# One number of the placement table: where VectorE normalises the second row block's differential heads

## The reference

```python
h = _rmsnorm(x, pre_norm_g[i])
z = h @ w_in[i]
qa, ka, va, qi, ki, wi, ga, qb, kb, vb, gb = _split_in(z)
qa = _partial_rope(...); ka = _partial_rope(...)      # 8 heads of 64, 16 columns rotated
oa = _dsa_attention(qa, ka, va, qi, ki, wi, top_k)    # top 64 keys of each query
qb = _partial_rope(...); kb = _partial_rope(...)
# (softmax(Q1 K1) - lam * softmax(Q2 K2)) V, then an RMS norm over each head's 128 columns
ob = _rmsnorm(_diff_out, subln_g[i]) * (1.0 - lam_init)
y = concatenate([oa * silu(ga), ob * silu(gb)]) @ w_out[i]
x = x + _rmsnorm(y, post_norm_g[i])
e = (p[i] @ w_ple_proj[i]) * sigmoid(x @ w_ple_gate[i])
x = x + _rmsnorm(e, ple_norm_g[i])
```

## Time and profile before

| | us |
|---|---|
| median of 3 runs (367.97 to 368.6) | 368.36 |
| the profiled execution's own time | 368.36 |
| its span | 366.6 |
| PE busy | 354.2 (97%) |
| DVE busy | 265.0 (72%) |
| ACT busy | 227.5 (62%) |
| POOL busy | 69.0 (19%) |

### The profile page before, as it was taken

One profiled execution on the slowest core, in us unless ns is written; L12 is line 12 of the kernel. 1 busy time (PEld: TensorE's weight loads), 2 busy tenths in 40 slices (PEclk: granted clock), 3 DMA queues, 4 the chain that ended last, 5 costly groups with the idle time before them and its releaser, 6 DMA issues.

```text
span 366.6 us, 5649 instructions
## 1 busy us (share of the span) xinstructions
PE 354.2 (97%) x1908; PEld 291.9 (80%) x1908; DVE 265.0 (72%) x554; ACT 227.5 (62%) x455; POOL 69.0 (19%) x121
## 2 busy tenths in 40 slices
PE   7799999999999999999999999999999999999992
PEld 6597788788887878888888877878888788888881
DVE  2666798879975586687697478878997658668543
ACT  4667565875867953664584547588586795366221
POOL 1514522023600000004005612203360000000000
PEclk9899999999999999999999999999999999999998
DMA  7999836354585364467754845646457436540011
GB/s 255 319 217 322 308 116 183 116 160 130 166 239 169 116 194 163 154 214 138 213 168 139 279 121 167 172 117 176 121 168 244 154 115 219 165 161 32 0 53 63
DMA packets 32076, 61.65 MB, mean 168 GB/s; under 512 B 2384, under 2 KB 4688, under 8 KB 32048
## 3 DMA queue, kind: packets, MB, share of 16 engines
q1 hardware_dynamic: 30928, 58.01, 50.3%
q0 software_dynamic: 1120, 3.28, 4.4%
HBM read 60.23 MB, written 1.05 MB: 167 GB/s over the span
## 4 chain that ended last, share of the span: by engine, by line
PE 90%; issue 2%; DMA 2%; POOL 2%; DVE 1%; ACT 1%; SPq 0%; DVEq 0%; POOLq 0%
PE proj L983 26%; PE proj L985 25%; PE proj L984 25%; PE sc L1087 3%; PE sc L1028 3%; PE tr L1100 2%; DMA g_norm<-in_pre_norm_g_dram 2%; PE tr L1044 2%; PE pv L1121 2%; PE pv L1116 1%; PE sc L1058 1%; POOL v_all L470 1%; DVE work L755 0%; DVE w_lo L716 0%; PE tr L1035 0%
## 5 line engine op out<-in xcount | busy, mean ns | idle before, releaser
L983 PE MATMUL proj<-w_hi,act_hi 128*128 128x512 f32 (+1 forms) x416 | 166.2, 400 | 0.2 <-DVE act_lo L768 0.2
L985 PE MATMUL proj<-w_hi,act_lo 128*128 128x512 f32 (+1 forms) x416 | 160.3, 385 | 0.0
L984 PE MATMUL proj<-w_lo,act_hi 128*128 128x512 f32 (+1 forms) x416 | 159.8, 384 | 0.0
L716 DVE TENSOR_TENSOR w_lo<-raw,w_hi 128x1024 fp32r<-128x1024 f32 (+1 forms) x108 | 129.4, 1213 | 21.3 <-ACT w_hi L529 20.4
L529 ACT ACTIVATE w_hi<-raw 128x1024 fp32r<-128x1024 f32 (+1 forms) x108 | 109.4, 1032 | 5.8 <-DMA raw<-in_w_in_dram 4.0
L983 PEld LDWEIGHTS proj<-w_hi,act_hi 128*128 128x128 f32 x416 | 78.2, 188 | 16.2 <-issue 1.1
L985 PEld LDWEIGHTS proj<-w_hi,act_lo 128*128 128x128 f32 x416 | 78.1, 188 | 15.9
L984 PEld LDWEIGHTS proj<-w_lo,act_hi 128*128 128x128 f32 x416 | 78.3, 188 | 12.9
L477 POOL TENSOR_TENSOR rstd<-var,minus_half 128x1 f32<-128x1 f32 x12 | 6.7, 554 | 183.8 <-DVE var L706 168.6
L630 ACT ACTIVATE probs<-probs,neg_max 128x128 f32<-128x128 f32 (+1 forms) x64 | 28.2, 446 | 3.3 <-DVE neg_max L839 3.2
L529 ACT ACTIVATE pT<-tr 128x512 f32<-128x512 f32 (+1 forms) x22 | 12.7, 575 | 17.4 <-PE tr L1100 15.5
(11 more groups left out here) (126 smaller groups left out, 390.9 us busy)
## 6 DMA issues: line engine op xcount, KB each, us to landing
raw<-in_w_in_dram SPq DMA_DIRECT2D x64, 512.0 KB, 3.9
raw<-in_w_out_dram SPq DMA_DIRECT2D x16, 512.0 KB, 3.3
raw<-in_w_ple_gate_dram SPq DMA_DIRECT2D x16, 512.0 KB, 3.6
raw<-in_w_in_dram SPq DMA_DIRECT2D x8, 324.0 KB, 6.8
raw<-in_w_ple_proj_dram SPq DMA_DIRECT2D x4, 512.0 KB, 3.5
resid<-in_x_dram SPq DMA_DIRECT2D x2, 512.0 KB, 7.3
g_norm<-in_post_norm_g_dram POOLq DMA_DIRECT2D x2, 512.0 KB, 6.0
g_ple<-in_ple_norm_g_dram POOLq DMA_DIRECT2D x2, 512.0 KB, 7.1
```

The lines of the kernel that those rows point to most:

```text
L716: nc.vector.tensor_tensor(w_lo[:, g % SLOTS, 0:nk * cols], raw[:, g % RAW_SLOTS, 0:nk * cols], w_hi[:, g % SLOTS, 0:nk * cols].bitcast(fp3 ...
L983: nc.tensor.matmul(ps, src_hi[:, b, k0 + k, :], hi, start=(first_u and k == 0), stop=False)
L984: nc.tensor.matmul(ps, src_hi[:, b, k0 + k, :], lo, start=False, stop=False)
L985: last = nc.tensor.matmul(ps, src_lo[:, b, k0 + k, :], hi, start=False, stop=last_k)
```

## The change

One number. The step `hn` of row block 1 moves from behind piece 29 to behind piece 31, in both layers.

```diff
     hv=[21, 27],
-    hn=[23, 29],
+    hn=[23, 31],
     topk=[[0, 0, 2, 6, 6, 7, 10, 11], [12, 24, 24, 25, 26, 26, 27, 31]],
```

## The result

| | before | after |
|---|---|---|
| median of 6 runs each, on one chip, us | 368.48 | 370.94 |
| lowest to highest | 367.77 to 369.20 | 370.09 to 371.37 |
| ratio, 95% interval | | 1.0065 [1.0049, 1.0083] |
| the profiled execution, us (span) | 368.36 (366.6) | 371.55 (369.8) |

The changed kernel is slower by 2.46 us. The forecast was 370.5, in a range of 369.7 to 371.3.

The account below looks back on a forecast made before the run. PE was taken to bound the kernel from 30 us on. Moved normalisation 0, earlier subtractions 0, a PE stop of 1.09 us in each of two layers: 368.36 + 2.2 = 370.5 us, range 369.7 to 371.3.

Parts of the forecast that it names:

- What bounds: From 30 us to the last matmul PE sets the time, and any stop of PE is kept to the end.
- The moved normalisation: On DVE, five operations of 1.23 us end some 2.5 us later; PE needs them twelve pieces later; cost 0.
- The subtractions earlier: On DVE, two subtractions start 1.23 us earlier; the transfers and matmuls they release have nobody waiting; gain 0.
- The rotation's delay: On POOL, two subtractions meet the rotation of KA's block 0 and add 2.06 us to it.
- The stop: PE's transposes of KA's block 0 start at 99.11 instead of 98.02: 1.09 us lost in each layer.
- The first start: DVE starts at 95.31, POOL at 95.36; if POOL is first, the stop differs by a tenth.
- the pair of subtractions of the earlier trace: Two DVE subtractions taking 2.54 us, set against 2.85 beside POOL's second rotation to show that they stretched.
- The upper bound: Longest holds on POOL's rotation, its third operation held too: 2.31 us delay, 1.34 stop, 2.7 for both layers, 371.0.
- the longer wait: A held POOL operation goes on only about 115 ns behind DVE's end; 1.2 us more for both layers, 371.7; not adopted.
- keep its turn: Rival: only the rotation's first operation is held, about 1.0 us, PE late by a few hundredths, 368.4; chance 0.09.
- The second rotation: POOL's rotation of KA's block 1 loses its 1.79 us of delay; rival faster by 0 to a few tenths, chance 0.02.
- The clock: Rival: PE's granted clock falls behind the stop, about 1.7 us more lost a layer, about 374; chance 0.04.

Follow-up runs that it names:

- Experiment 4: The kernel before with the normalisation moved to 31 in layer 0 alone, layer 1 left at 29: 369.98 us, ratio 1.0037.
- experiment 3: The changed kernel with PE's transposes of KA's block 0 one piece later (KA=[34, 37]): 369.05 us, ratio 1.0004.
- experiment 2: The kernel before with the normalisation moved to 33, three more DVE steps later than in the changed kernel: 371.23 us, ratio 1.0074.

## Why the prediction was right

**What bounds.** PE, once the start is over, and it keeps every stop. Experiment 4 shows the adding, and experiment 3 that nothing but PE's stops counts. "From 30 us on" was read off one trace: in six of the ten PE waits for a `w_lo` between 31 and 34 us, so the start reaches a little further.

**The moved normalisation, cost 0.** Right: experiment 2 moves it further at no price.

**The subtractions earlier, gain 0.** Right as far as it shows: experiment 3 has them as early as the changed kernel, without the stops, and stands at 1.0004.

**The rotation's delay.** Forecast 2.06 us, read off another pair in the trace; measured 3.56 - 1.54 = 2.02. **The stop:** forecast 1.09 in each layer, measured 1.05 and 1.04, the 0.15 from POOL to PE included. The first start, with DVE ahead by 0.03 to 0.05, went to DVE in every trace that has the new order; POOL first was not met. One comparison of the prediction has a wrong base: the pair of subtractions of the earlier trace rows runs beside a rotation too. Where POOL does nothing, in the kernel before, a pair takes 2.35:

```profile
129.84 2.35 DVE L716 TENSOR_TENSOR w_lo<-raw,w_hi 128x1024 fp32r<-128x1024 f32 x2
```

Beside a rotation pairs take 2.54, 2.62 and 2.85, so POOL lengthens a pair by 0.2 to 0.5; the exclusion goes both ways, as the prediction says, and its sum doesn't use this number. The upper bound let `scale_h` hold the rotation's third operation; that one was plain (0.31), and `scale_h` was the one that took longer.

On when the held operation goes on, the rows speak against the longer wait. The first subtraction alone has this row in the changed kernel:

```profile
96.31 1.21 DVE L716 TENSOR_TENSOR w_lo<-raw,w_hi 128x1024 fp32r<-128x1024 f32 x1
```

It ends at 97.52. The operation of POOL that it holds ends at 97.85, so its own 0.46, if that is its plain time once it goes on, began at 97.39, or 0.13 ahead of the reported end. The Trainium skill (SBUF — State Buffer, "A bandwidth-pool intuition that's wrong (but worth ruling out)") gives about 115 ns behind the end, a figure measured on a DMA's descriptor generation. For these two compute engines the trace doesn't agree: by it each of two holds would be 0.25 longer and the rotation's delay about 2.5, where 2.02 was measured. The prediction took 199.86 for the end of the subtraction in the earlier trace rows, as half of a pair whose second half is the longer; the difference is a few hundredths and changes nothing in this.

**The total.** 2.18 forecast, 2.46 measured, with an interval of 1.8 to 3.1. The 0.3 between them has no place in the traces, where the two landmarks of the table lie 2.22 further apart, and it is within the noise: against the two larger sets of the kernel before, 369.00 and 368.42, the 31 runs on record of the changed kernel, median 370.81, are slower by 1.8 and 2.4. That the forecast is right to a few tenths is therefore worth less than that each of its terms was found.

**The rivals.** The rotation doesn't keep its turn: two operations in a row are held. The second rotation was freed, as expected, and nobody waits for it. The clock did not fall in the stop, in which PE, long busy before, paused for about 1 us; here is the stretch of the earlier trace rows in the changed kernel, where PE lost 0.90 of busy time and the granted clock stayed at 1.00:

```profile
95.00:110.00 15.00, 14.10 (x77) 11.22 (x76) 13.78 (x35) 8.78 (x18) 4.97 (x8) 1.00 0.70 204
```

## What to carry to other kernels

Before moving work on VectorE, put GpSimd's timeline beside it. Here a 128x1024 subtraction with two SBUF inputs and an operation of GpSimd took turns (each operation held by a whole subtraction lasted 0.8 to 1.1 us longer), while a normalisation that reads PSUM and a multiplication that writes its sum left GpSimd at its plain times. So a move that leaves both queues' work unchanged can still lengthen a chain on the other engine. Look for who waits soonest behind what is newly hit, and compare the slack there with the delay; here 1.1 us of slack stood against 2.0 of delay, and with one instruction less in the way 0.08 us was lost in each layer, with one matmul piece more of slack nothing. Where a clash can't be avoided, let it fall on the operation that is needed last.

## What the runs showed of the hardware that I had not expected

A multiplication of a 128x1024 tile by a constant, in float32 from SBUF to SBUF, took 1.55 us for two, against 2.62 for two subtractions in the same place, and held POOL for 0.50 and 0.45 us although it has one SBUF input. The same multiplication with its sum written out took 1.21 each and held nothing. I had left both outcomes open for the plain form. The Trainium skill (SBUF — State Buffer, "Who interferes with whom") names just these two forms: a `tensor_scalar` can run in the fast mode that takes the port pair shared with GpSimd, except in the form that also writes out its accumulator. Both rows agree.

The start of this kernel varies more than its middle. The transposes of QB's block 0 begin between 48.31 and 50.43 us in the traces that have the same instructions up to there. In the traces of before and after, whose first 40 us run the same instructions, PE waited for the second unit's `w_lo` 2.2 and 2.8 us, and in that of experiment 3 it waited at 32.85 once more for 1.1, a wait that the trace before doesn't have:

```profile
32.85 0.50 PE L983 MATMUL proj<-w_hi,act_hi 128*128 128x512 f32 x1 [1.06 <-DVE w_lo L716]
```

The comparison of two spans is good to two microseconds only, therefore; the waits by place are good to a few hundredths. What makes the start vary was not tried.
